# One product of the recurrence moved from VectorE to GpSimd, and the expert result's halves signalled apart, in a two-block network kernel on one core

## The reference

```
u = rmsnorm(x, ln1_w[l]);  proj = u @ w_in[l]
o_a = rwkv7_mixer(zr, zk, zv, zw, za, zg, ...)      # a recurrence over 256 tokens, 8 heads of 64
o_b = nsa_mixer(...);  o_c = swa_sink_mixer(...)
x = x + (g_a*(o_a @ w_br_a) + g_b*(o_b @ w_br_b) + g_c*(o_c @ w_br_c)) @ w_out
x = x + peer_ffn(rmsnorm(x, ln2_w[l]), ...)         # per token: 8 heads x 16 experts of 16384
```

## Time and profile before

| What | Value |
|---|---|
| Runs | 3980.76, 3974.51, 3980.33 us; median 3980.33 us |
| Profiled execution | 3971.93 us |
| Its span, first to last instruction | 3970.1 us |
| PE, DVE, ACT, POOL busy | 3676.1, 2549.3, 1593.2, 692.5 us |
| Granted clock of TensorE, mean | 0.98 |

### The profile page before, as it was taken

The page is one execution under the profiler, slowest core; times in us unless marked ns, Lnnn a source line. Parts: engine busy times, 40 slices in busy tenths (PEclk is TensorE's granted clock), DMA queues, the critical chain, the costliest instruction groups (busy, mean ns, idle before and its releaser), DMA issues. The chain is left out here.

```text
span 3970.1 us, 66133 instructions
## 1 busy us (share of the span) xinstructions
PE 3676.1 (93%) x25476; PEld 3174.1 (80%) x25476; DVE 2549.3 (64%) x5098; ACT 1593.2 (40%) x3567; POOL 692.5 (17%) x698
## 2 busy tenths in 40 slices
PE   8999989999999998999899999878889999998887
PEld 6888766788788876898778899777777798987776
DVE  4878547677755566655546767676564567776774
ACT  5222537323232334543235444444332354444443
POOL 0010002000000002000000244443300003454442
PEclk9999999999999999999999999999999999999999
DMA  6555211355433420444134799999942268999998
GB/s 260 197 196 182 74 47 54 108 186 182 150 117 138 138 97 22 170 182 170 71 112 175 274 419 420 421 421 420 421 167 78 105 224 334 420 419 420 421 421 330
DMA packets 135194, 909.48 MB, mean 229 GB/s; under 512 B 14807, under 2 KB 16087, under 8 KB 34016
## 3 DMA queue, kind: packets, MB, share of 16 engines
q0 software_dynamic: 93952, 615.72, 38.6%
q1 hardware_dynamic: 40928, 289.53, 20.2%
HBM read 904.11 MB, written 5.28 MB: 229 GB/s over the span
## 5 line engine op out<-in xcount | busy, mean ns | idle before, releaser
L2824 PE MATMUL ps<-arena 128*128 128x128 f32 x6560 | 838.3, 284 | 148.5 <-ACT arena L2887 148.1
L2824 PEld LDWEIGHTS ps<-arena 128*128 128x128 f32 x6560 | 794.6, 197 | 199.7 <-ACT arena L2887 192.6
L3001 POOL DMA_INDIRECT arena<-peer_uv,arena x410 | 445.8, 1087 | 1383.2 <-DVEq L2962 792.7
L709 DVE TENSOR_TENSOR w_lo<-wt,w_hi 128x1024 fp32r<-128x1024 f32 x389 | 476.5, 1225 | 314.0 <-ACT w_hi L691 288.5
L3029 DVE CUSTOM_DVE_ANT_0 arena<-arena 128x1024 f32<-128x1024 f32 x410 | 502.4, 1226 | 271.0 <-DMA arena<-peer_uv,arena 265.5
L744 PE MATMUL ps<-h_hi,w_hi 128*128 128x512 f32 (+1 forms) x1744 | 644.0, 371 | 6.7 <-ACT h_hi L937 3.5
L691 ACT ACTIVATE w_hi<-wt 128x1024 fp32r<-128x1024 f32 x389 | 408.7, 1060 | 579.8 <-PE ps L744 548.7
L744 PE MATMUL ps<-h_hi,w_lo 128*128 128x512 f32 (+1 forms) x1744 | 634.5, 366 | 0.0
L744 PE MATMUL ps<-h_lo,w_hi 128*128 128x512 f32 (+1 forms) x1744 | 593.1, 365 | 0.5 <-DVE h_lo L957 0.5
L744 PEld LDWEIGHTS ps<-h_hi,w_hi 128*128 128x128 f32 x1744 | 331.1, 190 | 65.3 <-issue 10.3
L744 PEld LDWEIGHTS ps<-h_hi,w_lo 128*128 128x128 f32 x1744 | 331.0, 190 | 54.6 <-issue 1.9
(11 more groups left out here) (361 smaller groups left out, 5344.2 us busy)
## 6 DMA issues: line engine op xcount, KB each, us to landing
wt<-wstream SPq DMA_DIRECT2D x245, 1024.0 KB, 4.8
ada_t<-adastream POOLq DMA_DIRECT2D x128, 512.0 KB, 3.6
arena<-wstream SPq DMA_DIRECT2D x18, 1024.0 KB, 7.8
arena<-adafirst SPq DMA_DIRECT2D x8, 1024.0 KB, 15.5
arena<-peer_uv,arena POOLq DMA_INDIRECT x410, 19.1
arena<-bias_by_query POOLq DMA_DIRECT2D x2, 3072.0 KB, 15.4
bias_by_query<-bias_by_distance POOLq DMA_DIRECT2D x1, 4096.0 KB, 19.5
xT<-tokens SPq DMA_DIRECT2D x2, 1024.0 KB, 6.2
```

The costliest lines, as they stand in the source:

```text
L709: self.step(self.dve.tensor_tensor(lo, raw_group(g), hi.bitcast(F32), ALU.subtract))
L2824: ins = pe.matmul(y_banks(t)[m // 4][:, (m % 4) * P:(m % 4 + 1) * P], row[:, D + m * P:D + (m + 1) * P], diag[n % DIAGS], start=s == 0 and ...
L3001: pool.indirect_dma_start(out=rows[at % GB], out_offset=None, in_=peer_uv, in_offset=bass.IndirectOffsetOnAxis(ap=experts[:, t, s:s + 1], ...
```

## The change

The product `rt` is no longer made by VectorE behind the fourth chain. GpSimd makes it as soon as it is past the barrier ahead of the core's stage, and raises a new semaphore, `decayed`; TensorE waits for that before `("br", 0)`, in place of its second wait on `late_ready`. Second, in `pe_peer`, the fourth of the eight matmuls of a tile's last slot (the last into the first bank) raises a new semaphore, `half_done`. In `dve_peer_out`, VectorE waits for `half_done` ahead of the first addition, and for `row_free` only ahead of the second; before, it waited for `row_free` ahead of both.

```diff
@@ pe_rwkv_core
                         if (name, of) == ("br", 0):
-                            pe.wait_ge(late_ready.sem, late_ready.due(pe))
+                            pe.wait_ge(decayed.sem, decayed.due(pe))
                         gram(*grams[name], of)
@@ dve_rwkv_core
                     level_of(t, g, 1)
                     dve.sem_inc(level_ready.sem, 1)
-            step(dve.tensor_tensor(rt, zr, pcum, ALU.mult))
-            dve.sem_inc(late_ready.sem, 1)
             for level in range(1, LEVELS):
@@ pe_peer
                     for m in range(DC):
+                        if s == SLOTS - 1 and m == 4:
+                            ins.then_inc(half_done.sem, 1)
                         ins = pe.matmul(y_banks(t)[m // 4][:, (m % 4) * P:(m % 4 + 1) * P], row[:, D + m * P:D + (m + 1) * P],
@@ dve_peer_out
-            dve.wait_ge(row_free, done)
             for half, bank in enumerate(y_banks(t)):
+                if half:
+                    dve.wait_ge(row_free, done)
+                else:
+                    dve.wait_ge(half_done.sem, half_done.due(dve))
                 seg = xT[:, 4 * half:4 * half + 4, t * P:(t + 1) * P]
@@ GpSimd's list of stages
                     if n == 10 + l * 8:
                         pool_load_bias(pool, l)
+                    if n == 11 + l * 8:
+                        pool.tensor_tensor(rt, zr, pcum, ALU.mult).then_inc(decayed.sem, 1)
```

More of the change, by code:

```diff
@@ L1636, in model_kernel @@
         late_ready = signal("late_ready")
+        decayed = signal("decayed")
         level_ready, turned_ready = signal("level_ready"), signal("turned_ready")
@@ L2745, in model_kernel @@
         ztok_ready = signal("ztok_ready")
+        half_done = signal("half_done")
         subs_ready = signal("subs_ready")
```

## The result

The changed kernel took 3985.75 us (median of 20 runs), the kernel before on the same chip 3977.55 us (20 runs). The ratio is 1.002, with a 95% interval of 1.0014 to 1.0027: slower by 8.2 us, where I had forecast 1.8 us less. The time lies inside the stated range, 0.25 us from its upper end, but the sign is wrong.

A forecast was written before the change was run, and what follows sets the result against it. It took TensorE, busy for 93% of the span, to set the pace where the product ran; 2 x 0 - 2 x 0.92 = -1.8 us took 3980.3 to 3978.5 us, chance 0.47, range 3973 to 3986.

The forecast's parts named there:

- the stated range: Whole kernel's time: 3973 to 3986 us, with 0.90 given to a result within 0.2%.
- I take 0 by these rows: Core's first chain: GpSimd's product beside VectorE's instructions holds none of them up, 0 us.
- The first rival: Core's first chain: GpSimd's product holds VectorE up, 1.9 us a layer; +2.0 us in all, 3982.3 us; chance 0.38.
- GpSimd starts 0.24 us after VectorE: Behind the barrier ahead of the core: GpSimd starts 0.24 us later than VectorE, so `kt` goes first.
- the removed product is worth 0: Core, behind the fourth chain: taking the product off VectorE gains 0, since TensorE's run of matmuls covers it.
- the wait for `decayed` costs 0: Core's second level, ahead of `("br", 0)`: TensorE's wait costs 0, the product being wanted almost 20 us after the barrier.
- the halves: Each layer's end of the experts: the first addition starts under the remaining matmuls; -0.92 us a layer, 1.84 in both.
- the 2.6 that I took: GpSimd's product in the core: its own time taken as 2.6 us, inside ends of 1.54 and 5.3 us.
- The bound of 0.2%: Whole kernel: a difference under 0.2%, or 8 us, can hardly be told from none; slower than that 0.05.

The follow-up runs named there:

- memset_beside: Kernel before plus a GpSimd memset, which reads nothing, at the place of the moved product; 3971.16 us (one run).
- kept_on: Changed kernel plus a thrown-away 128x512 product on TensorE ahead of each wait for the last two chains; 3967.99 us, ratio 0.9996 to the kernel before.
- halves_kept_on: halves_only_3 plus a thrown-away 128x512 product on TensorE ahead of the last chain; 3967.55 us, ratio 0.9992 to the kernel before.
- product_after_kt: Changed kernel, but GpSimd waits ahead of its product until VectorE has made kt; 3972.43 us, ratio 1.0006 to the kernel before.
- no_product: Kernel before without the product, so the recurrence reads the decay alone; 3971.03 us (one run).
- product_late_3: Changed kernel, but GpSimd starts its product only when VectorE is through the four chains; 3966.46 us, ratio 0.9995 to the kernel before.
- halves_only_3: Kernel before with only the expert result's halves signalled apart, the product staying on VectorE; 3967.16 us, ratio 0.9995.
- product_only_3: Kernel before with only the product moved to GpSimd, both additions waiting as before; 3977.66 us, ratio 1.002.
- after_again: The repeat: the changed kernel unaltered, measured once more; 3974.03 us, ratio 1.0012 to the kernel before.

## Why the prediction was wrong

- **Wrong: "I take 0 by these rows" for what the product does to VectorE.** The first rival took place, and at my own size: 1.9 us a layer foretold, 1.36 and 2.21 us measured, paid in full at the last turn as I had said. What failed is the weighing. L1541 has two values a partition, and I called it weak evidence, yet let it carry the choice. The 410 dot products ran beside GpSimd's gathers, not beside GpSimd arithmetic. Neither row showed the pair in question at its size.
- The Trainium skill, "SBUF — State Buffer", section "Who interferes with whom", states the rule that I set aside: a VectorE instruction with two SBUF inputs and a GpSimd instruction that reads SBUF exclude each other for a whole instruction. The traces agree in both orders (VectorE first by a hair: 0.42 to 1.78 us for L1901, GpSimd 3.45 instead of 2.37; GpSimd first: `kt` 1.23 to 3.44 us), and with its exception for GpSimd instructions that only write (`memset_beside`, 0.96 us beside an unchanged 1.23). The 0.16 us of L1541, inside a GpSimd instruction of 1.8 us, do not fit the rule, and no run here says why.
- **Missing: a term for TensorE's clock.** The first rival ended at +3.8 - 1.8 = +2.0 us. The measured core gives +9.5 - 1.8 in one trace, and +5.3 - 1.8 in the other of the same kernel. What lies above 3.6 us of hold is 5.9 us in the one, 1.7 us in the other. That the clock does it is shown for the first layer's first level by `kept_on`, against three traces without the thrown-away products. That it is always so was not shown, and `halves_kept_on` speaks against an easy use of it.
- **Wrong: GpSimd starts 0.24 us after VectorE.** The earlier trace rows have a transfer there, not arithmetic. The product started 0.00 us after VectorE's in one layer and 0.01 us ahead in the other, and the order decides which VectorE instruction is held up: with `kt` let go first (`product_after_kt`), it is the first-level mask in both layers.
- **Right: the removed product is worth 0** (`no_product`, to 0.2 us), because TensorE sets the pace there; VectorE's idle time ahead of the first `ka` mask is 1.69 us in `product_late_3`, against 0.32 before. **Right: the wait for `decayed` costs 0**: the product is ready at 1903.37, some 19 us before its use. **Right: the halves, -0.90 us a layer** for the -0.92 worked out, by the traces; the median of `halves_only_3` is too near to no change to bear it out. **Right in size: GpSimd's own 2.37 us** for the 2.6 that I took. The Trainium skill, "GPSIMD Engine Reference", section 3.1, gives 4497 ns for an addition (not a product) of 2048 values; half of it is an estimate of 2.25 us, which is nearer to the measured 2.37.
- **The bound of 0.2%**, about 8 us, was taken as out of reach; the loss of 8.2 us in the first measurement sits on it. The repeat, at 0.12%, is within. Their intervals overlap from 1.0014 to 1.0021. That the stated range still held 3985.75 us is luck: its upper end came from a GpSimd time of up to 5.3 us, which did not occur, and not from the clock, which did.

Open stays what decides where within the core the granted clock falls. Open, too, is the late start of the experts' dot products (some 4.5 us in both layers), seen in one of the changed kernel's two traces and in none of the other experiments'.

## What to carry to other kernels

Before work goes to GpSimd, look at what VectorE does in the same microseconds: if it sets the pace there with instructions that read two inputs from SBUF, much of the moved instruction's duration can be paid for (here 1.36 and 2.21 us of 2.37), by other VectorE instructions than the one relieved. The same product, released some ten microseconds later under a run of matmuls, cost nothing that could be measured, and gained nothing either, since VectorE was not the limit there. A row counts as evidence on contention only if both sides are of the kind and the size in question; and a delay ahead of TensorE may be charged twice, once as waiting and once in clock.

## What the runs showed of the hardware that was not expected

- Two engines behind one barrier started within 0.03 us of each other (0.01 us with the product on GpSimd). Which one then went first was the same in all four traces of the whole product at this place (the changed kernel twice, `product_only_3`, `kept_on`): VectorE in the first layer, where `kt` took 1.23 us, GpSimd in the second, where it took 3.44.
- A GpSimd instruction that waits is recorded as long: 3.45 us beside `kt`, where the same product took 2.37 us when it went first or when VectorE's instructions beside it had one input from PSUM.
- A VectorE delay of 1.36 us was followed by 192 matmul records at 6.09 instead of 4.91 us, the clock having gone to 0.50. TensorE had been idle for 1.21 and 1.49 us shortly before; in the kernel before 1.49 us of idle stood alone behind 48 unbroken matmul records, and the clock held. That is no rule: in the second layer of `after_again` 0.89 and 1.49 us of idle stood at this place, and the 10 us from 2970 had a clock of 1.00.
- The core of an untouched kernel came back to 0.02 us (52.66 / 51.31 and 52.66 / 51.33), while in the one trace with a GpSimd memset beside it the second layer's was 2.8 us longer, with low stretches of the clock and no hold.
